# Second weight tile of each stage's opening pair: its last 128 columns as three split products instead of full float32 ones

## The reference

```python
for l in range(2):                                     # first block
    h = layer_norm(ALPHA*h + 0.5*swiglu(h, ffn1_gate[l], ffn1_up[l], ffn1_down[l]))
    z = h @ w_in[l]                                    # cb, cc, ch, rq, rf, ri, rg, pu
    h = layer_norm(ALPHA*h + concat(conv, hgrn2, pool) @ w_out[l])
    h = layer_norm(ALPHA*h + cross_attn(h, mem, ca_q[l], ca_k[l], ca_v[l], ca_o[l]))
    h = layer_norm(ALPHA*h + 0.5*swiglu(h, ffn2_gate[l], ffn2_up[l], ffn2_down[l]))
proj = h @ w_in_2                                      # second block: xa, ga, q, k, v, go, glr, ma, mb
h = layer_norm(A2*h + (rg_lru(conv(xa)) and gla(q, k, v), gated) @ w_out_2)
h = layer_norm(A2*h + moe(h, 32 experts, top 4)); h = h + sigmoid(h @ w_ple_gate) * (p @ w_ple)
```

## Time and profile before

| | us |
|---|---|
| median of 3 runs | 2436.54 (2435.53 to 2437.04) |
| the profiled execution's own time | 2434.89 |
| its span in the profile | 2433.1 |
| PE busy | 2364.7 (97% of the span) |
| DVE busy | 1170.5 (48%) |
| ACT busy | 806.0 (33%) |
| POOL busy | 196.9 (8%) |

### The profile page before, as it was taken

One profiled execution on the slowest core, in us unless ns is written; L12 is line 12 of the kernel. 1 busy time (PEld: TensorE's weight loads), 2 busy tenths in 40 slices (PEclk: granted clock), 3 DMA queues, 4 the chain that ended last, 5 costly groups with the idle time before them and its releaser, 6 DMA issues.

```text
span 2433.1 us, 32509 instructions
## 1 busy us (share of the span) xinstructions
PE 2364.7 (97%) x13087; PEld 1620.3 (67%) x13087; DVE 1170.5 (48%) x1599; ACT 806.0 (33%) x1010; POOL 196.9 (8%) x94
## 2 busy tenths in 40 slices
PE   8999999999999999999999999999999999999998
PEld 7889989888888998888898973333333333333334
DVE  5567866755755876675676852211221111111114
ACT  4454344544444434444447322111111111111111
POOL 0002402200200250220020100000000000000000
PEclk9999999999999999999999999999999999999999
DMA  7664454555556545456546469999999999999994
GB/s 249 215 207 160 154 177 132 192 190 192 186 185 206 169 139 190 140 177 205 171 140 208 148 231 410 427 426 426 428 427 427 427 426 428 427 426 427 427 426 187
DMA packets 223800, 665.07 MB, mean 273 GB/s; under 512 B 9889, under 2 KB 164511, under 8 KB 191056
## 3 DMA queue, kind: packets, MB, share of 16 engines
q1 hardware_dynamic: 223696, 663.57, 71.7%
HBM read 662.50 MB, written 1.05 MB: 273 GB/s over the span
## 4 chain that ended last, share of the span: by engine, by line
PE 76%; DMA 18%; DVE 3%; ACT 2%; issue 1%; SPq 0%; DVEq 0%; ACTq 0%
PE ps L683 19%; DMA ring<-in_w_up_dram 17%; PE ps L694 14%; PE ps L668 10%; PE ps L1282 9%; PE ps L1326 6%; PE ps L779 5%; PE ps L1264 2%; PE ps L1255 2%; PE ps L887 2%; PE ps L1423 1%; PE ps L1304 1%; PE ps L1128 1%; PE ps L939 1%; PE ps L729 1%
## 5 line engine op out<-in xcount | busy, mean ns | idle before, releaser
L2034 DVE TENSOR_TENSOR ring_halves<-ring,ring_halves 128x2048 fp32r<-128x2048 f32 x206 | 510.5, 2486 | 207.9 <-ACT ring_halves L1505 207.8
L683 PE MATMUL ps<-x_halves,ring_halves 128*128 128x512 f32 (+1 forms) x2560 | 457.2, 339 | 0.0
L1505 ACT CAST ring_halves<-ring 128x2048 fp32r<-128x2048 f32 x206 | 392.9, 1907 | 131.9 <-PE ps L694 98.4
L683 PEld LDWEIGHTS ps<-x_halves,ring_halves 128*128 128x128 f32 x2560 | 394.4, 188 | 59.3
L1282 PE MATMUL ps<-ring,work 128*64 128x512 f32 x1536 | 344.0, 595 | 40.9 <-DMA ring<-in_w_up_dram 40.2
L2561 DVE TENSOR_SCALAR work<-work 128x128 f32<-128x128 f32 x64 | 19.3, 343 | 692.0 <-PE ps L1282 692.0
L694 PE MATMUL ps<-ring_halves,work_halves 128*128 128x512 f32 x1184 | 288.9, 391 | 0.2
L1282 PEld LDWEIGHTS ps<-ring,work 128*64 128x64 f32 x1536 | 106.6, 137 | 271.4 <-issue 195.5
L694 PEld LDWEIGHTS ps<-ring_halves,work_halves 128*128 128x128 f32 x1184 | 221.6, 188 | 47.1 <-issue 2.3
L668 PE MATMUL ps<-x_halves,ring_halves 128*128 128x256 f32 x2016 | 250.0, 285 | 0.0
L668 PEld LDWEIGHTS ps<-x_halves,ring_halves 128*128 128x128 f32 x2016 | 244.4, 192 | 0.9 <-issue 0.4
(11 more groups left out here) (277 smaller groups left out, 2171.3 us busy)
## 6 DMA issues: line engine op xcount, KB each, us to landing
ring<-in_w_up_dram SPq DMA_DIRECT2D x96, 2048.0 KB, 37.0
ring<-in_w_down_dram SPq DMA_DIRECT2D x33, 2048.0 KB, 37.1
work<-in_w_up_dram SPq DMA_DIRECT2D x32, 2048.0 KB, 35.5
work<-in_w_down_dram SPq DMA_DIRECT2D x31, 2048.0 KB, 40.0
ring<-in_w_in_dram SPq DMA_DIRECT2D x52, 1024.0 KB, 5.2
ring<-in_ffn_gate_dram SPq DMA_DIRECT2D x44, 1024.0 KB, 5.4
ring<-in_ffn_up_dram SPq DMA_DIRECT2D x44, 1024.0 KB, 5.4
ring<-in_ffn_down_dram SPq DMA_DIRECT2D x44, 1024.0 KB, 4.9
```

What stands on the lines that cost most here:

```text
L683: mm = pe.matmul(out, wt[:, o:o + P], x, start=(k == 0 and n == 0), stop=(k == DT - 1 and n == 1))
L1505: nc.scalar.copy(high_of(name)[:], ring[:, s, :]).then_inc(hi_done.add(name), 1)
L2034: v.tensor_tensor(ring_halves[s][:], ring[:, s, :], high_of(name)[:].bitcast(F32), ALU.subtract)\
```

## The change

Of the second tile b of each pair, the second 128 columns (`pt` 1) are now multiplied in split form. PE does b's first 128 columns in float32 as before, for t 0 and for t 1, and then waits for the split activations and for b's low part, and runs `column_strip`: 8 x 3 split matmuls over all 256 tokens. So `split_inputs` stands ahead of the strip now, and b waits on `lo_done`.

ACT's cast and DVE's subtraction for such a tile cover its second 128 columns only (`second_half`: 128 x 8 x 128). The tile b (rf1, cq1, up 0, xa1) enters the order of split tiles ahead of the others of its stage. With halves made three tiles ahead, the end of the stage before now makes those of b and of two further tiles, and what was the third (cc, co0, down 0, q0) is made inside the stage, by a new `next_high` and `next_low` each.

```diff
@@ -180,15 +180,15 @@
-ORDER_MIX1 = ("rq0", "rq1", "cc", "ch", "cb", "pu", "ri0", "ri1", "ck0", "ck1", "ck2", "ck3", "rg0", "rg1",
-              "cv0", "cv1", "cv2", "cv3", "wo0", "wo1", "wo2", "wo3", "cq2", "cq3", "co0", "co1", "co2", "co3")
-ORDER_MIX2 = ("xa2", "xa3", "q0", "q1", "k0", "k1", "v0", "v1", "v2", "v3", "go0", "go1", "go2", "go3",
+ORDER_MIX1 = ("rf1", "rq0", "rq1", "cc", "ch", "cb", "pu", "ri0", "ri1", "ck0", "ck1", "ck2", "ck3", "rg0", "rg1",
+              "cv0", "cv1", "cv2", "cv3", "wo0", "wo1", "wo2", "wo3", "cq1", "cq2", "cq3", "co0", "co1", "co2", "co3")
+ORDER_MIX2 = ("xa1", "xa2", "xa3", "q0", "q1", "k0", "k1", "v0", "v1", "v2", "v3", "go0", "go1", "go2", "go3",
               "mb0", "mb1", "mb2", "mb3", "ga0", "ga1", "ga2", "ga3", "ma0", "ma1", "ma2", "ma3")
...
-    out = []
+    out = [(tag, "up", 0)] if tag != ("f1", 0) else []
     for c in range(1, 9):
...
@@ -279,6 +279,8 @@
         place_of = {name: n for n, name in enumerate(order)}
+        half_split = {"xa1"} | {name for L in range(LAYERS) for name in
+                                (("rf1", L), ("cq1", L), (("f1", L), "up", 0), (("f2", L), "up", 0))}
...
@@ -310,6 +312,12 @@
             return ring_halves[WH + place_of[name] % 3]
+
+        def second_half(tile, name):
+
+            if name in half_split:
+                return tile.rearrange("p (k n) -> p k n", k=DT)[:, :, P:CH]
+            return tile
...
@@ -656,17 +664,22 @@
+            def column_strip(name, bank, pt, xhigh=xh, xlow=xl):
+
+                high, low = high_of(name), ring_halves[slot_of[name]]
+                for k in range(DT):
+                    o = k * CH + pt * P
+                    for n, (wt, x) in enumerate(((high, xhigh), (high, xlow), (low, xhigh))):
+                        mm = pe.matmul(ps[:, bank, pt * T:pt * T + T], wt[:, o:o + P], x[:, k, :],
+                                       start=(k == 0 and n == 0), stop=(k == DT - 1 and n == 2))
+                return mm
+
             def by_columns(name, bank, xhigh=xh, xlow=xl):
...
                 pe.wait_ge(lo_done.sem, lo_done.at(name))
-                high, low = high_of(name), ring_halves[slot_of[name]]
                 for pt in range(2):
-                    for k in range(DT):
-                        o = k * CH + pt * P
-                        for n, (wt, x) in enumerate(((high, xhigh), (high, xlow), (low, xhigh))):
-                            mm = pe.matmul(ps[:, bank, pt * T:pt * T + T], wt[:, o:o + P], x[:, k, :],
-                                           start=(k == 0 and n == 0), stop=(k == DT - 1 and n == 2))
+                    mm = column_strip(name, bank, pt, xhigh, xlow)
                 release(mm, name)
...
@@ -788,10 +801,13 @@
                 arrived(b_name)
-                half(b_name, b_bank, 0, (0, 1))
+                half(b_name, b_bank, 0, (0,))
                 turned_copied(tag, 1)
                 release(half(a_name, a_bank, 1, (0, 1)), a_name)
-                release(half(b_name, b_bank, 1, (0, 1)), b_name)
+                half(b_name, b_bank, 1, (0,))
+                split_inputs(tag)
+                pe.wait_ge(lo_done.sem, lo_done.at(b_name))
+                release(column_strip(b_name, b_bank, 1), b_name)
...
@@ -815,7 +831,8 @@
                     first_pair(before, (((tag, "gate", 0), 0), ((tag, "up", 0), 1)))
-                split_inputs(before)
+                if opening:
+                    split_inputs(before)
...
@@ -910,7 +927,6 @@
                 first_pair((0, L), ((("rf0", L), 0), (("rf1", L), 1)))
-                split_inputs((0, L))
                 by_columns(("rq0", L), 2)
...
@@ -1009,7 +1025,6 @@
                 first_pair((1, L), ((("cq0", L), 2), (("cq1", L), 3)))
-                split_inputs((1, L))
                 scores(0)
...
@@ -1044,7 +1059,6 @@
             first_pair((3, LAYERS - 1), (("xa0", 0), ("xa1", 1)))
-            split_inputs((3, LAYERS - 1))
             by_columns("xa2", 2)
...
@@ -1502,7 +1516,8 @@
                 act.wait_ge(loaded[s].sem, loaded[s].at(name))
-                nc.scalar.copy(high_of(name)[:], ring[:, s, :]).then_inc(hi_done.add(name), 1)
+                nc.scalar.copy(second_half(high_of(name)[:], name), second_half(ring[:, s, :], name))\
+                    .then_inc(hi_done.add(name), 1)
...
@@ -1595,6 +1610,8 @@
                 hidden(0)
+                if not opening:
+                    next_high((tag, "up", 0))
                 for c in range(1, 11):
...
@@ -1644,6 +1661,7 @@
                         .then_inc(emptied[j].sem, 1)
+                next_high(("rf1", L))
                 for j in range(2):
...
@@ -1735,6 +1753,7 @@
                 expo(0)
+                next_high(("cq1", L))
                 q_copy(2)
...
@@ -1775,7 +1794,7 @@
                 copy_out(j, xa[:, 2 * j:2 * j + 2, 3:259], ps[:, j, :].rearrange("p (g t) -> p g t", g=2))
-                if j >= 2:
+                if j >= 1:
                     next_high(f"xa{j}")
...
@@ -2031,7 +2050,8 @@
                 dve.wait_ge(hi_done.sem, hi_done.at(name))
-                v.tensor_tensor(ring_halves[s][:], ring[:, s, :], high_of(name)[:].bitcast(F32), ALU.subtract)\
+                v.tensor_tensor(second_half(ring_halves[s][:], name), second_half(ring[:, s, :], name),
+                                second_half(high_of(name)[:].bitcast(F32), name), ALU.subtract)\
                     .then_inc(lo_done.add(name), 1)
...
@@ -2149,6 +2169,8 @@
                 hidden(0)
+                if not opening:
+                    next_low((tag, "up", 0))
                 for c in range(1, 11):
...
@@ -2242,6 +2264,7 @@
                 mine(("k", L))
+                next_low(("rf1", L))
                 next_low(("rq0", L))
...
@@ -2326,6 +2349,7 @@
                 negmax(1)
+                next_low(("cq1", L))
                 next_low(("cq2", L))
...
@@ -2383,6 +2407,7 @@
             conv(0)
+            next_low("xa1")
             next_low("xa2")
...
             for nm in ("xa3", "q0", "q1", "k0", "k1", "v0"):
```

## The result

The changed kernel is slower: 2440.63 us against 2436.98 us for the kernel before, medians of 20 runs each, ratio 1.0014 (95% interval 1.0008 to 1.0020). That is some 3.5 us. The forecast was no change, 2436.4 us with a range up to 2440.0.

A forecast was written before the change was run, and what follows sets the result against it. PE, busy 97% of the span, was taken to bound the kernel. Savings at five openings less losses in two mixers and the second block gave -0.12 us; with the runs' median 1.65 higher, 2436.4 us, range 2433.2 to 2440.0.

The forecast's parts named there:

- What PE saves: At each opening pair, 16 float32 matmuls become a strip of 24 split ones: 0.70 us saved, 5.6 us for all eight.
- The covers: Spare time before PE wants its inputs: 0.24 us for t 1's copies, 0.63 for the tile behind the pair, 0.2 for down 0.
- The turns of DVE and POOL: Behind an opening, DVE and POOL alternate whole operations; the half subtraction (1.22 us for 2.28) brings later turns 1.06 us sooner.
- Rival 1: DVE and POOL share the port evenly, so DVE gains 1.84 us instead of 1.06: 2434.1 us; chance 0.09.
- The new waits: PE waits for low parts: about 1.9 us ahead of cc in each mixer, 1.3 us ahead of q0 in the second block.
- To this I add 0.15 for starting again: PE restarting after the new wait ahead of cc costs 0.15 us, making each mixer +1.34 us net; also used at q0.
- So they move along: Second block's later PE waits for DVE at L887 (3.5 us together) follow ACT work that PE releases, so they shift with it.
- The sum: Five openings at -0.70 us, two mixers at +1.34 and the second block at +0.70 give -0.12 us.
- Rival 2: Thin covers at t 1's copies, the first tile and down 0 fall short by tenths: +2.4 us, 2438.8 us; chance 0.12.
- rival 3: The half subtraction on DVE costs a whole one, 2.28 us, so DVE gains nothing: +7.2 us, 2443.7 us; chance 0.06.
- rival 4: The openings' full 5.6 us gain arrives, with no wait ahead of cc: 2430.9 us; chance 0.04.
- rival 5: The strip's matmuls run no faster than float32, so five openings save nothing: +3.4 us, 2439.9 us; chance 0.03.

## Why the prediction was wrong, step by step

- **What PE saves: nearly right.** The strip takes 2.88 us (24 of the 168 records in 20.16), as worked out. The float32 part takes 7.22 instead of 7.15. The profile has no wait there; that the copies of t 1, with 0.24 us to spare on paper, cost the 0.07 is a guess. Per opening 0.63 instead of 0.70, and 0.5 to 0.64 from A to A.
- **The covers: right.** No wait ahead of the strip, the tile behind the pair or down 0, at any of the eight.
- **The turns of DVE and POOL: right.** The half subtraction cost 1.22 us and all behind it came 1.07 earlier (1.06 foreseen). Rival 1, which had 1.84 us earlier, falls. The Trainium skill (SBUF — State Buffer, "SBUF: two separate sides") has it that the port pair is held for whole instructions; the rows of 4.45 and 4.50 us beside a 1.22 agree.
- **The new waits: right.** 1.94 us twice and 1.31 us, foreseen 1.9 and 1.3.
- **The step that failed: "To this I add 0.15 for starting again".** That was all that starting again was to cost, and 0.1 of it came from no row. With the clock up it measured 0.14 us and another 0.23 by which cc takes longer (5.98 for 5.75), so that mixer 1 lost 1.51 us against 1.34. Where the clock fell, another 1.6 us came on top: mixer 0 lost 3.02 against 1.34. The second block lost 2.1 against 0.70, with 1.7 of it behind its old 2.6 us wait. I had taken the clock as full over the whole span, by its mean of 0.998, and the one 2.6 us wait without a fall as the rule. The full clock was a misreading. The trace of the kernel before shows two falls among the experts. At the first, PE is recorded as busy, though just ahead of it with 7 records in two microseconds where dense stretches have 12; the second stands behind a PE wait of 0.91 us:

```profile
1494.00:1496.00 2.00, 2.00 (x7) 1.00 0.99 426
1496.00:1498.00 2.00, 2.00 (x10) 0.56 0.98 418
1498.00:1500.00 2.00, 2.00 (x8) 0.59 1.06 451
```

```profile
2396.86 1.51 PE L1437 MATMUL ps<-ident,hn 128*128 128x128 f32 x8 [0.91 <-DVE hn L2662]
```

```profile
2396.00:2398.00 2.00, 1.15 (x8) 0.84 0.51 205
2398.00:2400.00 2.00, 1.99 (x4) 0.50 0.05 12
```

  They should have put a price on new waits: a stretch at half clock, which measured some 1.6 us in a run of dense matmuls.
- **"So they move along", of the waits at L887: half right.** The longer wait kept its 2.6 us, but got a fall of the clock behind it. The shorter one fell from 0.94 to 0.67 us where cc's low part is early and q0's is not. That is why q0, which begins 0.67 us later as foreseen (0.70), costs the second block only 0.45.
- **The sum.** Foreseen -0.12 us. Two falls add 3.3 and the smaller gain of five openings 0.5: +3.7, as the stretches sum to, and measured some 3.5. None of the five rivals had it. Rival 2 asked for two or three tenths at each thin cover, where one gave 0.07 at most; rival 3 for a half subtraction of 2.28 us, which took 1.22; rival 4 for no wait ahead of cc; rival 5 for a strip no faster than float32.

The forecast of no change by the bound of 0.2% still holds (0.14%). But the range ended at 2440.0, and 2440.63 lies above it: waits and turns were foreseen rightly, the clock was not in the sum.

## What to carry to other kernels

Where an engine is busy 97% of the time, work taken off it is worth only what the next releaser can follow: here eight times 0.63 us came in, and three new waits of 1.3 to 1.9 us took it back. Two of them go when one subtraction stands ahead of other work on DVE, the third with another. Making work for the feeding engine early matters more than the order in which it was natural to write it: the changed kernel with that one line moved is the faster one, by 3.9 us over before. And a short new wait of TensorE in dense work should be priced twice, at its length, and at its length plus a stretch of half clock. Useless matmuls that fill it show which of the two it is, as long as the profile is searched for falls elsewhere too: one of those here came and went with edits some 90 us or more ahead of it.

## What the runs showed of the hardware that I had not expected

Behind a wait of 1.94 us TensorE's granted clock fell to 0.50 shortly after work had begun again, in four of four profiles, at a cost of some 1.6 us (cc 7.48 us for 5.98). The same wait in the other mixer had no fall in four of four; at 4.33 us both had one. With the same wait filled by matmuls there was none. A kernel with useless work on the engine in place of idling was 3.3 us faster, 1.6 of it at the filled wait; the other 1.7 were a fall behind a 2.6 us wait further on, which wasn't filled. A low part that came just in time, without a wait in the profile, still cost a mixer 0.3 us.
